# Where the operands lie in a partition: a two-layer backbone step with opH and opL moved behind the weights

## The reference

```python
h = rms_norm(x, p['norm_w'][li, 0]) * (1 + sc1) + sh1
y = even_layer(h)            # or odd_layer(h)
x = x + g1 * y
h = rms_norm(x, p['norm_w'][li, 1]) * (1 + sc2) + sh2
x = x + g2 * (jnp.square(jax.nn.relu(h @ w1)) @ w2)
```

## The kernel before

| tile | starts before | starts after |
|---|---|---|
| opH, opL | 28,800 and 41,152 | 131,072 and 143,424 |
| raw, wH, wL | 53,504, 86,272 and 102,656 | 28,800, 61,568 and 77,952 |
| nbuf, ident, ones | 119,040, 123,648 and 124,160 | 94,336, 98,944 and 99,456 |
| hidH, hidL | 130,976 and 143,264 | 155,776 and 168,064 |
| hq, vtok, dv | 143,264, 176,960 and 159,648 | 118,560, 124,704 and 106,272 |
| QK, att | 149,408 and 183,104 | 155,776 and 183,328 |

## Time and profile before

### The profile page before, as it was taken

The page is one execution under the profiler, slowest core; times in us unless marked ns, Lnnn a source line. Parts: engine busy times, 40 slices in busy tenths (PEclk is TensorE's granted clock), DMA queues, the critical chain, the costliest instruction groups (busy, mean ns, idle before and its releaser), DMA issues.

```text
span 1047.8 us, 17863 instructions
## 1 busy us (share of the span) xinstructions
PE 1020.6 (97%) x7330; PEld 941.7 (90%) x7330; DVE 568.5 (54%) x914; ACT 486.1 (46%) x858; POOL 140.8 (13%) x173
## 2 busy tenths in 40 slices
PE   6999999999999999999999999999999999999997
PEld 3888885778999999999997989886999999999997
DVE  5556676564744345354457576576465445345452
ACT  5544665664553342342344556667464234252342
POOL 0162200011010010110110342350001011010110
PEclk9999999999999999999999999998999999999999
DMA  9987719645435445445445532223223524333311
GB/s 330 343 283 244 237 48 322 202 162 195 152 121 167 155 161 161 161 159 162 153 129 186 176 104 68 86 87 101 80 81 121 162 92 149 120 120 120 121 41 61
DMA packets 156974, 160.44 MB, mean 153 GB/s; under 512 B 3146, under 2 KB 155108, under 8 KB 156900
## 3 DMA queue, kind: packets, MB, share of 16 engines
q1 hardware_dynamic: 154512, 156.15, 45.0%
q0 software_dynamic: 704, 1.97, 0.6%
q10 hardware_dynamic: 1684, 1.26, 0.4%
HBM read 156.09 MB, written 3.28 MB: 152 GB/s over the span
## 4 chain that ended last, share of the span: by engine, by line
PE 92%; DVE 3%; ACT 2%; issue 1%; DMA 1%; SPq 0%; DVEq 0%; ACTq 0%
PE G L585 63%; PE G L590 13%; PE OB L607 4%; PE TB L554 4%; PE SC L918 2%; PE OB L932 1%; PE SC L694 1%; DMA raw<-in_w_ada 1%; PE OB L715 1%; PE OB L785 1%; PE TB L900 1%; ACT wH L1024 1%; PE SC L670 1%; PE SC L664 1%; PE SC L626 1%
## 5 line engine op out<-in xcount | busy, mean ns | idle before, releaser
L585 PE MATMUL G<-opH,wH 128*128 128x386 f32 (+1 forms) x768 | 267.7, 349 | 1.1 <-DVE wL L1505 0.8
L1024 ACT ACTIVATE wH<-raw 128x2048 fp32r<-128x2048 f32 x94 | 179.6, 1911 | 180.9 <-PE G L585 178.1
L585 PE MATMUL G<-opH,wL 128*128 128x386 f32 (+1 forms) x768 | 260.4, 339 | 0.0
L585 PE MATMUL G<-opL,wH 128*128 128x386 f32 (+1 forms) x768 | 260.2, 339 | 0.0
L1505 DVE TENSOR_TENSOR wL<-raw,wH 128x2048 fp32r<-128x2048 f32 x94 | 215.8, 2296 | 42.9 <-ACT wH L1024 42.9
L585 PE MATMUL G<-hidH,wH 128*128 128x384 f32 x512 | 173.3, 338 | 0.0
L585 PE MATMUL G<-hidH,wL 128*128 128x384 f32 x512 | 172.1, 336 | 0.0
L585 PE MATMUL G<-hidL,wH 128*128 128x384 f32 x512 | 172.1, 336 | 0.0
L585 PEld LDWEIGHTS G<-opH,wH 128*128 128x128 f32 x768 | 144.9, 189 | 9.8 <-issue 5.4
L585 PEld LDWEIGHTS G<-opL,wH 128*128 128x128 f32 x768 | 144.8, 189 | 1.6
L585 PEld LDWEIGHTS G<-opH,wL 128*128 128x128 f32 x768 | 144.9, 189 | 0.0
(11 more groups left out here) (246 smaller groups left out, 1192.6 us busy)
## 6 DMA issues: line engine op xcount, KB each, us to landing
raw<-in_w_mlp SPq DMA_DIRECT2D x64, 1024.0 KB, 5.2
raw<-in_w_ada SPq DMA_DIRECT2D x48, 1024.0 KB, 7.0
raw<-in_w_in_even SPq DMA_DIRECT2D x13, 1024.0 KB, 7.2
raw<-in_w_in_odd SPq DMA_DIRECT2D x12, 1024.0 KB, 5.1
raw<-in_w_out_even SPq DMA_DIRECT2D x4, 1024.0 KB, 6.6
raw<-in_w_out_odd SPq DMA_DIRECT2D x4, 1024.0 KB, 5.0
xin<-in_x_sample SPq DMA_DIRECT2D x2, 512.0 KB, 5.7
out_y_sample<-yout SPq DMA_DIRECT2D x1, 768.0 KB, 4.1
```

The costliest lines, as they stand in the source:

```text
L585: mm = pe.matmul(G[:, s, 512 * m:512 * m + cols], w[:, s, k, P * m:P * m + P], a[:, k, 0:cols], start=first and q == 0, stop=last and q == 2)
L1024: act.activation(wH[:, u % 2, :, :], raw[:, pos % RAW, :, :], ACT.Copy).then_inc(w_high, 1)
```

## The change

opH and opL leave their place ahead of the weights and are entered behind all fixed tiles and behind a new block `lower_arena` of 6200 floats (PAD = 56 of them). In that block four short lists share storage: F, hq and vtok of layer 0; xin; yout, relu and relu2 of the MLPs; dv and doT of layer 1. The other tiles of the old lists stay in lists behind opL. No instruction, wait or transfer is added, taken away or moved in its engine's order; only the addresses differ.

```diff
--- before.py
+++ after.py
@@ -64,6 +64,7 @@
 ADA_COLS = 24
 SH1, SC1, G1, SH2, SC2, G2 = range(6)
 NX = NTOK + 2
+PAD = 56
 MLP0_ORDER, MLP1_ORDER = [4, 5, 0, 1, 2, 3, 6, 7], list(range(KT))
 
 
@@ -272,8 +273,6 @@
 
 
         xT = sb("xT", [P, KT, NTOK])
-        opH = sb("opH", [P, KT, NX], F32R)
-        opL = sb("opL", [P, KT, NX], F32R)
         raw = sb("raw", [P, RAW, KT, UC])
         wH = sb("wH", [P, 2, KT, UC], F32R)
         wL = sb("wL", [P, 2, KT, UC], F32R)
@@ -300,14 +299,29 @@
                 h.__exit__(None, None, None)
             return got
 
-        xin, vrow0, vrow1 = arena([("xin", [P, TT, D], F32), ("vrow0", [P, P], F32), ("vrow1", [26, P], F32)])
-        (F, hq, QK, T37, vtok, att, qout, kout, vout, qT, kT, PB, PT, obuf, S0, swaK, swaV, ropeE, masks,
-         wmask, idbf, att32, mask32) = arena([
+        (F, hq, vtok) = arena([
             ("F", [P, 2, 12, P], F32),
             ("hq", [P, 12, P], F32),
+            ("vtok", [P, TT, 512], F32)])
+        (xin,) = arena([("xin", [P, TT, D], F32)])
+        (yout, relu, relu2) = arena([
+            ("yout", [P, TT, D], F32),
+            ("relu", [P, 2, 2 * NTOK], F32),
+            ("relu2", [P, 2, 2 * NTOK], F32)])
+        (dv, doT) = arena([
+            ("dv", [P, TT, D], F32),
+            ("doT", [P, H_C, NTOK], F32)])
+        sb("lower_arena", [P, 6144 + PAD])
+
+
+        opH = sb("opH", [P, KT, NX], F32R)
+        opL = sb("opL", [P, KT, NX], F32R)
+
+        vrow0, vrow1 = arena([("vrow0", [P, P], F32), ("vrow1", [26, P], F32)])
+        (QK, T37, att, qout, kout, vout, qT, kT, PB, PT, obuf, S0, swaK, swaV, ropeE, masks,
+         wmask, idbf, att32, mask32) = arena([
             ("QK", [P, 4, 12, P], F32),
             ("T37", [P, 24 * 31], F32),
-            ("vtok", [P, TT, 512], F32),
             ("att", [P, 12, P], F32),
             ("qout", [P, TT, 512], F32),
             ("kout", [P, TT, P], F32),
@@ -326,13 +340,10 @@
             ("idbf", [P, P], BF16),
             ("att32", [P, 6, 32], F32),
             ("mask32", [P, 5, 32], U8)])
-        hidH, hidL, relu, relu2, yout = arena([("hidH", [P, KT, NTOK], F32R), ("hidL", [P, KT, NTOK], F32R),
-                                         ("relu", [P, 2, 2 * NTOK], F32), ("relu2", [P, 2, 2 * NTOK], F32),
-                                         ("yout", [P, TT, D], F32)])
-        (dqT, dkT, dv, dkc, dvc, draw, dsq, dout, DP, DW, DPT, doT, ropeO, lamp) = arena([
+        hidH, hidL = arena([("hidH", [P, KT, NTOK], F32R), ("hidL", [P, KT, NTOK], F32R)])
+        (dqT, dkT, dkc, dvc, draw, dsq, dout, DP, DW, DPT, ropeO, lamp) = arena([
             ("dqT", [P, H_C, NTOK], F32),
             ("dkT", [P, H_C, 512], F32),
-            ("dv", [P, TT, D], F32),
             ("dkc", [P, D], F32),
             ("dvc", [P, D], F32),
             ("draw", [P, 2, 768], F32),
@@ -341,7 +352,6 @@
             ("DP", [P, 2, 2, NTOK], F32),
             ("DW", [P, 2, NTOK], F32),
             ("DPT", [P, NTOK], F32),
-            ("doT", [P, H_C, NTOK], F32),
             ("ropeO", [P, 2, 2, 2, HD], F32),
             ("lamp", [P, 4, HD], F32)])
 
```

## The result

The changed kernel takes 1051.64 us, the median of 20 runs (1048.84 to 1054.73), against 1049.39 for 20 runs of the kernel before beside it: ratio 1.0022, 95% interval 1.0012 to 1.0032. That is 2.3 us slower, where 9 us faster was forecast. The profiled execution of after has a span of 1047.3 us (1049.49 with what lies around it) and is one of its quicker ones, while that of before had the clock dips at 170 to 235 and 720 to 767. So the two spans, 1047.8 and 1047.3, can't show the 2.3 us; the runs do, and the traces show which stage differs. All lines of after stand 10 further down (585 is 595, 590 is 600).

A forecast was written before the change was run, and what follows sets the result against it. TensorE's matmul starts were taken to bound the kernel from 60 us on. Gains of 4.6 + 1.8 + 2.7 - 0.4 (lost in waits) + 0.2 = 8.9 us gave 1040.2 us, range 1034.5 to 1045.5.

The forecast's parts named there:

- What bounds the kernel: From 60 us on, the distance between starts of TensorE's matmuls; a nanosecond there counts some 5,000 times.
- They collide when both lie below byte 131,072: In the matmul streams, next stationary and present moving factor collide if both lie low; costs op 3.0 ns a matmul.
- a fixed start can't make the same tile's matmuls scatter from 332 to 346: Argument from op's matmul durations against the rival that blamed block pitch or length; that rival's chance was 0.09.
- the address doesn't matter, the pitch does: Rival for op's products: block pitch of 1544 bytes or length 386 costs the 3 ns; no change, 1049.2 us, chance 0.09.
- fm with 386: In the two MLPs, 1536 matmuls with 386 columns of op each lose 3.0 ns: 4.6 us gained.
- fm with 384: 768 matmuls with 384 columns of op pace at 173.4 instead of 175.8 ns: 1.8 us gained.
- small products: Attention and recurrence: at most some 150 float32 products gain up to 3 ns, 0.5 us; 0.2 us taken.
- tok: Products with op as stationary factor: 1008 matmuls after the first 60 us gain 2.7 ns each, 2.7 us.
- Weight loads from above are slower: Rival: op as stationary factor loads slower from above 131,072, 200 against 188 ns; 8.5 us slower, 1057.7 us, chance 0.04.
- fixed remainder: Lower bound for 256-column products: hid's 13.4 ns beyond its columns is fixed, giving 120.1 ns, 2.4 us lost.
- fm gains, tok loses: Rival: products with op moving gain, those with op stationary lose 2.4 us; 4.0 us gained, 1045.2 us, chance 0.12.
- The other engines: ScalarE, VectorE and GpSimd accesses at new addresses cost nothing, since these engines run in TensorE's shadow.

The follow-up runs named there:

- e4: Changed kernel with 128 unused bytes ahead of raw, putting it back on a multiple of 256; weights move 128 bytes, op and hid stay: 1050.38 us against 1049.42, ratio 1.0011.
- e2: Kernel before with hidH and hidL given op's block pitch, 386 columns of which 384 are used: 1052.14 us against 1049.42, ratio 1.0037.
- e5: No step, only streams of 48 matmuls on TensorE alone, varying starts, pitch, length and half: 8.32 / 48 = 173.3 to 176.7 ns by start at 384 columns.
- e3: Kernel before with 128 unused bytes ahead of raw, so raw and all tiles behind it move up 128 bytes: 1052.60 us against 1049.42, ratio 1.0035.
- e6: Changed kernel with raw alone moved to a 256-byte boundary; weights, op and hid keep their places modulo 512: 1049.59 us against 1049.90, ratio 1.0000.
- e1: Kernel before with op's blocks 392 columns apart instead of 386, only 386 used: 1049.60 us against 1049.42, ratio 1.0002.
- e9: As e7, but opH and opL start 64 bytes lower, hid keeping its place: 1047.29 us against 1048.54 for the kernel before, ratio 0.9979.
- e8: No step, only whole fm units of 386 columns in 48 placings of op against the weights: 175.4 to 177.9 ns a matmul in second units.
- e7: As e4, with hidH and hidL also moved up 128 bytes: 1047.70 us against 1048.67 for the kernel before, ratio 0.9991.

## Why the prediction was wrong

**What bounds the kernel** held: the distance between matmul starts, from 60 us on. So did the comparison of 173.4 with 177.2, and that 3.0 ns needed a cause.

**"They collide when both lie below byte 131,072"** is the step that failed. With opH at 131,072 op paces at 177.2 ns as it did at 28,800. hid and op differ in their half, but also in pitch, in length and in where they start against the weights. I kept the first and dropped the second with "a fixed start can't make the same tile's matmuls scatter from 332 to 346". That is false as it stands: with a pitch of 1544 bytes there is no one start. The eight blocks start 8 bytes further each time against a weight tile whose own pieces step evenly, so the pairs differ. And where there is one start a stream can scatter even so: e4's hid has a pitch of 1536, its blocks and the weights' all start at the same place modulo 256, and its durations run from 335 to 343. So the scatter, which the prediction took for the mark of two streams in one half, is no such mark. e2 gave the scatter to hid by the pitch alone, in the other half; e5 has equal paces in both halves. The rival "the address doesn't matter, the pitch does", with 0.09, named both causes that e5 shows, the start of the blocks and the length of 386, and was right for the products. Its first half was wrong: the half doesn't matter, the low bits of the address do (e4, e5).

The Trainium skill, "TensorE: Matmul & The Clock Gate", Part 2, speaks for separate read ports of the weight load and the moving factor. The prediction took the paces of before as evidence against that. No half played a part, but e4 and e5 still don't fit the sentence that loading the next weights takes nothing from the running matmul: the weights' own address changes the pace, from 173.4 to 175.9 ns for hid in e4 and by 1.6% at start 0 in e5. Which read waits for which no run shows.

**fm with 386, fm with 384, small products** (4.6 + 1.8 + 0.2 us): nothing came of any, as op kept its place of (128, 192) against the weights. Twelve of the small products of line 664 take 1.34 us in after as in the earlier trace rows. And op, now loaded from above 131,072 in tok, takes 189 ns a load where it took 188, so the rival "Weight loads from above are slower" is out too.

**tok** (2.7 us): nothing either, 117.9 instead of 118.1 ns. The term rested on the same collision, and e5 shows none for this form either: 120.0 ns low and 119.8 high with blocks 384 apart. That is the "fixed remainder" end of the bounds (120.1), and with op's 386 it is faster, 118.5, not slower. What the rival "fm gains, tok loses" had against it, a disturbed pace better than the undisturbed one, is what e5 shows of the pitch.

**What I left out of the list.** The part headed "The other engines" puts new addresses at nothing and names tiles that ScalarE, VectorE and GpSimd touch. raw, which moved from 53,504 to 28,800, and what writes it, the DMA queue, isn't in it, though the windows had the DMA share at 1.00 in the first 60 us, so any cost there had no cover. e3 makes that loss in the kernel before, e6 takes it out of the kernel after, and within the 1.3 us of e6's interval no other edit is needed for the 2.3 us. The Trainium skill, "DMA: Bandwidth & Descriptors", How a descriptor splits into AXI transactions, has the rule: a descriptor that doesn't start on a multiple of 256 bytes begins with the boundary below, and the bytes ahead of its start still cost beats. By its counting a packet of 1024 bytes, 128 past a multiple, takes 36 beats instead of 32, an estimate of 12.5% more; the medians of 46 and 51 ns in the first 30 us show 11%, the 48.8 and 50.4 ns over the whole run 3%. The page tells it of reads, here it is the written side.

How the slow packets turn into 2.3 us is only in part shown. They start the products late, and the runs with raw beside a multiple of 256 also have a lower granted clock: 0.9929 on the mean over the 20 runs of after and over e3's 7, against 0.9950 over the 26 runs of before beside e3 and 0.9948 over e6's 12. Among those 26 runs a straight line gives 0.66 us more for each 0.001 of clock less, so some 1.4 us of the loss go with the clock, an estimate. Both come and go with raw's start; how much each would cost alone stays open.

**Still open:** why one placing can have two paces. In e1 and e3, hid ran whole groups at 173.4 and others at 176.7, alternating 174 and 179, with the same addresses. It isn't the placing by itself: e5's streams at the same places (start 160 with the weights at 0 for e1, start 32 with the weights at 128 for e3) take 8.32 and 8.34 us, the fast pace. What a group inherits from the one before it may decide; in e5 the one stream that changed its pace between the passes had the same stream before it, and only the two short products in between were wider. More was not tried. By the same token e3's and e1's totals hold a share that their edit doesn't explain.

## What to carry to other kernels

When tiles are moved, list every tile's start modulo 256 before and after, those that only a DMA writes too: in a stage with a full queue there was nothing to hide the cost. When two streams of one kernel differ in pace, list all in which they differ before choosing a cause, and ask whether a constant named against a rival really is constant over the stream. The placing of both factors was worth 0.2% here, with raw on a multiple of 256 (e9), and a small kernel of streams alone (e8) found it.

## What the runs showed of the hardware beyond that

The pace of a one-pass matmul stream depends on the low address bits of both factors: 173.3 to 176.7 ns at 384 columns, 175.4 to 177.9 at 386 in e8's placings. What two columns more cost hangs on the pitch too: in e5, from start 0, 3.1 ns with blocks 512 apart, 1.0 with 386 and nothing with 416, where their own length is 0.8. The half of the partition is without effect (low and high within 0.03 us in 48 matmuls). From start 0 and with blocks 384 apart, 256 columns take 120.0 ns and 384 columns 173.3, both 13.3 above their columns at 2.4 GHz. While the queue was full, in the first 30 us, packets of 1 KB took 46 ns on a multiple of 256 bytes and 51 beside it (medians); from 60 us on the median was 46 in both. And the clock differed in after's start: TensorE, busy for 14.05 of the first 24 us, was granted 0.50 from 24 to 30 us, which is the 1.2 GHz level, where before, busy for 14.34, had 1.00:

```profile
24.00:30.00 6.00, 5.50 (x37) 3.31 (x39) 4.38 (x15) 2.21 (x6) 0.00 (x0) 0.50 1.10 348
```

This dip isn't tied to the slow packets alone: e4, e7 and e9, with packets of 46 ns, had 0.70 to 0.72 there. Nor is the clock alone the late start: in e3 and e6 this stretch had nearly the same clock, 0.62 and 0.66, and the fm start was 62.57 with the slow packets and 61.60 with the fast ones.
